# Expert layers: the hidden rows of two steps transposed together, the down products one step later

## The reference, cut to what matters

```python
def swiglu(h, w_gu, w_down):
    g, u = jnp.split(h @ w_gu, 2, axis=-1)
    return (jax.nn.silu(g) * u) @ w_down
...
# D_MODEL = 1024, SEQ = 256, N_EXPERTS = 8, TOP_K = 2, FFN_EXPERT = 3584
```

## Time and profile before

| | |
|---|---|
| median of 3 executions | 3080.19 us (3072.54, 3080.19, 3086.84) |
| the profiled execution | 3076.05 us, of it 3074.0 us span |
| TensorE busy | 2939.0 us, 96% of the span |
| VectorE busy, ScalarE busy | 1206.1 us (39%), 715.0 us (23%) |
| data read from HBM | 682.52 MB, 222 GB/s over the span |
| the expert stage | about 769 to 1740 us |
| mean granted clock of TensorE | 0.97 of full speed |

### The profile page before, as it was taken

How to read it: one execution, slowest core, us unless ns; L and a number is a source line. 1 busy time by engine, 2 the same in 40 slices (tenths; PEclk the granted TensorE clock), 3 DMA queues, 4 the chain that set the end, 5 groups by cost and what they waited for, 6 DMA issues and landing times.

```text
span 3074.0 us, 52144 instructions
## 1 busy us (share of the span) xinstructions
PE 2939.0 (96%) x23648; PEld 2023.6 (66%) x23648; DVE 1206.1 (39%) x2121; ACT 715.0 (23%) x1145; POOL 48.3 (2%) x39
## 2 busy tenths in 40 slices
PE   8888999998999999999999899899999999988898
PEld 6778988877233333333333466699999985687898
DVE  4767853242001111101101267455454543454454
ACT  2224432141000000000000111434334422311443
POOL 0000000000000000000000000000000000032000
PEclk9899999999999999999999999899999998998999
DMA  8756754537898999999999312046665331010452
GB/s 343 272 219 248 277 217 178 215 114 281 339 374 355 369 372 352 366 365 371 360 358 369 135 69 96 1 176 236 246 245 194 140 135 41 1 72 1 165 191 83
DMA packets 95204, 687.01 MB, mean 223 GB/s; under 512 B 10624, under 2 KB 11776, under 8 KB 11904
## 3 DMA queue, kind: packets, MB, share of 16 engines
q1 hardware_dynamic: 94400, 681.36, 57.6%
q10 hardware_dynamic: 576, 2.25, 0.2%
HBM read 682.52 MB, written 1.05 MB: 222 GB/s over the span
## 4 chain that ended last, share of the span: by engine, by line
PE 90%; DVE 5%; ACT 2%; DMA 1%; issue 1%; POOL 0%; SPq 0%; DVEq 0%; ACTq 0%
PE ps L493 40%; PE ps L1976 19%; PE ps L853 11%; PE ps L1999 7%; PE ps L764 5%; PE ps L2002 3%; PE ps L506 2%; PE ps L1984 1%; PE ps L739 1%; DMA ring<-W 1%; DVE FR L835 0%; DVE macc L609 0%; DMA XT<-XIN 0%; DVE AR L2472 0%; DMA sml<-SM 0%
## 5 line engine op out<-in xcount | busy, mean ns | idle before, releaser
L1976 PE MATMUL ps<-AR 128*32 128x512 f32 x4080 | 533.5, 592 | 0.0
L493 PE MATMUL ps<-HT,ring 128*128 128x256 f32 (+1 forms) x1696 | 443.4, 422 | 3.8 <-ACT HT L700 3.8
L493 PEld LDWEIGHTS ps<-HT,ring 128*128 128x128 f32 x1696 | 325.1, 193 | 115.4 <-issue 73.6
L493 PE MATMUL ps<-FR,FR 128*128 128x256 f32 x3120 | 390.1, 285 | 2.1 <-DVE M_moe_mod L617 1.7
L493 PEld LDWEIGHTS ps<-FR,FR 128*128 128x128 f32 x3120 | 379.8, 192 | 11.1 <-issue 8.6
L2087 DVE TENSOR_TENSOR AR<-AR,ps 128x256 f32<-128x256 f32 x84 | 35.5, 423 | 800.8 <-ACT AR L2051 800.8
L853 PE MATMUL ps<-FR,FR 128*128 128x256 f32 x2832 | 349.3, 283 | 0.0
L1976 PEld LDWEIGHTS ps<-AR 128*32 128x32 f32 x4080 | 150.7, 110 | 296.9 <-issue 294.5
L835 DVE TENSOR_TENSOR FR<-ring,FR 128x2048 fp32r<-128x2048 f32 x129 | 294.2, 2290 | 131.1 <-ACT FR L819 131.1
L853 PEld LDWEIGHTS ps<-FR,FR 128*128 128x128 f32 x2832 | 343.9, 192 | 0.8 <-issue 0.8
L819 ACT ACTIVATE FR<-ring 128x2048 fp32r<-128x2048 f32 x129 | 244.4, 1905 | 114.1 <-PE ps L853 86.7
(11 more groups left out here) (418 smaller groups left out, 2613.1 us busy)
## 6 DMA issues: line engine op xcount, KB each, us to landing
ring<-W SPq DMA_DIRECT2D x441, 1024.0 KB, 6.2
AR<-W SPq DMA_DIRECT2D x205, 1024.0 KB, 8.3
XT<-XIN ACTq DMA_DIRECT2D x2, 1024.0 KB, 8.6
cst<-CS SPq DMA_DIRECT2D x1, 1851.0 KB, 14.1
out<-XT SPq DMA_DIRECT2D x4, 256.0 KB, 2.2
sml<-SM SPq DMA_DIRECT2D x1, 970.5 KB, 10.2
cst<-CS ACTq DMA_DIRECT2D x1, 129.5 KB, 7.7
sml<-SM ACTq DMA_DIRECT2D x1, 16.0 KB, 5.2
```

The source lines that it names most:

```text
L493: ins = g.matmul(out, l, r, **kw)
L1976: ins = g.matmul(bank.ap[group(i), :], mo.hg[e % 2][:, 4 * h + k, group(t)], w[n][:, k, :], start=j == 0 and k == 0, stop=j == 1 and k == ...
```

## The change

Two consecutive steps' hidden rows are transposed together. The two `hu` buffers, 256 columns each, are read by one `turn` of four transposes at every second step (steps 2, 4, ..., 84), in place of two transposes at every step. They go to one PSUM bank, and one VectorE copy of 128x512 moves them into one half of a doubled buffer `hid2`, where the four `hid` buffers now are views. The down products of a round come three steps after its last piece and not two, so the loop has one step more, `scatter` comes one step later, and the `moe_d` loads move back by a step in SyncE's order. VectorE's `up` waits for the turn of the pair.

```diff
 def down_rounds(step):
-    return [n for n in range(ROUNDS) if last_up(n) == step - 2]
+    return [n for n in range(ROUNDS) if last_up(n) == step - 3]
...
     # expert_slots(), and the loops of TensorE, ScalarE and VectorE
-    for step in range(UPS + 2):
+    for step in range(UPS + 3):
...
-        mo.hid = [m_.get(256, "p (k j) -> p k j", k=2) for _ in range(4)]
+        mo.hid2 = [m_.get(512) for _ in range(2)]
+        mo.hid = [mo.hid2[i // 2][:, i % 2 * 256:i % 2 * 256 + 256].rearrange("p (k j) -> p k j", k=2) for i in range(4)]
...
         def scattered_at(e):
-            return last_up(14 * e + 13) + 4
+            return last_up(14 * e + 13) + 5
...
             # TensorE
             def turn(b):
                 bank = counts.take(p + ".turn", b)
-                s.wait_emptied(bank).wait_ge(p + ".hu", b)
-                for k in range(2):
-                    ins = g.transpose(bank.ap[:, k * 128:k * 128 + 128], mo.hu[b % 2][:, k * 128:k * 128 + 128], ident)
+                s.wait_emptied(bank).wait_ge(p + ".hu", b + 1)
+                for k in range(4):
+                    ins = g.transpose(bank.ap[:, k * 128:k * 128 + 128], mo.hu[k // 2][:, k % 2 * 128:k % 2 * 128 + 128], ident)
                 ins.then_inc(*s.done(p + ".turn", b))
             def down(n):
...
-                s.wait_ge(p + ".hd", last_up(n))
+                s.wait_ge(p + ".hd", last_up(n) // 2 * 2)
...
                 if step < UPS:
                     up(step)
-                if 1 <= step <= UPS:
-                    turn(step - 1)
+                if 2 <= step <= UPS and step % 2 == 0:
+                    turn(step - 2)
...
             # VectorE (its loop changes as TensorE's)
             def up(b):
                 s.wait_ge(p + ".sg", b)
                 if b >= 2:
-                    s.wait_ge(p + ".turn", b - 2)
+                    s.wait_ge(p + ".turn", (b - 2) // 2 * 2)
...
             def turn(b):
                 s.wait_ge(p + ".turn", b)
                 if b >= 4:
-                    s.wait_ge(p + ".down", (4 * (b - 4) + 3) // 3)
-                g.tensor_copy(mo.hid[b % 4], counts.bank(p + ".turn", b)[:, 0:256].rearrange("p (k j) -> p k j", k=2)).then_inc(
-                    *s.done(p + ".hd", b, empties=(p + ".turn", b)))
+                    s.wait_ge(p + ".down", (4 * (b - 3) + 3) // 3)
+                g.tensor_copy(mo.hid2[b % 4 // 2], counts.bank(p + ".turn", b)[:, :]).then_inc(*s.done(p + ".hd", b, empties=(p + ".turn", b)))
```

## The result

The changed kernel takes 3067.21 us (median of 11 executions, 3063.32 to 3071.11), the kernel before 3077.14 us (11 executions, 3070.36 to 3086.84). The ratio is 0.9966, with a 95% interval from 0.9954 to 0.9977: 0.34% faster, 10 us, with 7 to 14 us in the interval. I had forecast 7.7 us, and 3070.5 us. The profiled execution of the changed kernel has a span of 3065.7 us against 3074.0, 8.3 us less.

What follows compares the result with a forecast made beforehand. TensorE's instruction stream was taken to bound the expert stage; -12.2 + 2.8 + 1.7 = -7.7 us. This gave 3068.4 or 3072.5 us depending on the base, so 3070.5 us was forecast, range 3060 to 3081.

Steps and rivals of the forecast that it cites:

- a turn of two: TensorE's expert stage before the change: two transposes at a step, with the gap ahead of them, cost 0.51 us.
- a turn of four: TensorE's even steps after the change: four transposes cost 0.73 us, 0.22 more than two.
- gain in TensorE's stream: Expert stage: 84 turns of 0.51 us go and 42 of 0.73 come, -12.2 us.
- the delay and the moved loads: Down products and 112 `moe_d` loads one step later in SyncE's order: nothing moves, 0 us.
- the preparations behind that copy: VectorE's `prep` queued behind the larger copy, tightest at step 18: taken as nothing, bounds 0 and 1.4 us.
- wait for the accumulator bank: End of expert 0: `up(14)` takes the bank of `acc[0]` while ScalarE copies it out, +2.8 us once.
- half clock behind it: After expert 0's pause TensorE runs 3.3 to 3.4 us at 1.2 in place of 2.4 GHz, +1.7 us.
- the gap goes away with the transposes: Steps without a turn: down products follow up products at ordinary pace; otherwise 0.29 us stays in 42 steps.
- no stall: Rival, end of expert 0: the stall is hidden or absent, full -12.2 us, 3066 us; chance 0.12.
- It doesn't do what it says: Rival: the up-to-down gap stays in 42 steps without a turn, 0.29 us each, about 3082 us; chance 0.07.
- The stall at every end: Rival: every expert end but the last stalls with a clock fall, +19.3 us, about 3097 us; chance 0.04.
- The clock in the turns: Rival: each of 42 turns of four lets the clock fall, 71 us, about 3142 us; chance 0.01.

Runs made afterwards that it cites:

- the run with seven stalls: Changed kernel with the bank counter set, after experts 0 to 6, to that expert's first accumulator bank; 3087.50 us against 3078.17 for the kernel before, ratio 1.0030.
- the first experiment: Changed kernel with the bank counter moved on by two ahead of step 14, avoiding expert 0's accumulator banks; 3066.59 us against 3078.54 for the kernel before.
- eight in a row: Rows of four steps turned together, eight transposes every fourth step, one weight place less, no accumulator collision; 3055.31 us against 3078.17 for the kernel before.
- two turns in a row: Kernel before with the delay and two separate turns in even steps, bank counter moved on ahead of steps 24 and 66; 3066.11 us against 3078.54.

## Why the prediction was right, point by point

| step of the prediction | predicted | measured |
|---|---|---|
| a turn of two | 0.51 us | before: 9.95 - 9.44 |
| a turn of four | 0.73 us | 10.17 - 9.44 = 0.73 |
| a step without a turn | 9.44 us | 9.44 |
| gain in TensorE's stream | 12.2 us | 12.10 (stage without the stall) |
| the delay and the moved loads | 0 | 0.01 (stage) |
| VectorE's copy | 0.70 us, hidden | 0.68, hidden |
| the preparations behind that copy | 0 (at most 1.4 us) | 0: 5.9 us of idle weight loader ahead of their transposes in both kernels |
| wait for the accumulator bank | 2.8 us, once | 2.69, once |
| half clock behind it | 1.7 us | 1.73, the rest of 4.42; 1.70 from two up parts |
| sum | -7.7 us | -7.68 (stage) |

What carried it was the pace. An up part of 16 groups gave the price of a group, and two kinds of steps gave the turn's price with it. The row of waits would have misled: 70.4 us stand there for 84 gaps, and only 84 x 0.29 = 24 us of that could ever be had.

The step with the least ground was that the gap goes away with the transposes. No step of the kernel before showed up products followed by down products directly. The rows of down to up decided it, and the odd steps of the changed kernel show it.

The second was the bank. It is in no view of the profile of before, since there the wait doesn't exist. It came out of a walk through the allocation, and the price from the copies' rows. The place, the length and the one occurrence were right. Its clock term was right in this kernel but held for too sure: the run with seven stalls has the fall at three of seven. Had it not fallen, the sum would have been 9.4 us. That it fell at this pause, in the profiled execution, and the sum came out to 0.02 us, is in part luck.

The measured total moved by 10 us, not by 7.7. The forecast lies in the interval, 7 to 14 us. In the profiled executions the stage starts between 769.25 and 773.81 us, in nine kernels in which TensorE has the same work up to there. That is a scatter of 4.6 us ahead of TensorE's first changed step, more than the 2.3 us that differ. It goes with the clock outside the stage: of the changed kernel's eleven executions the three fastest (3063.3 to 3063.8 us) had a mean granted clock of 0.975, the two slowest (3071.0 and 3071.1 us) 0.970 and 0.971. That the 2.3 us are this scatter is likely and not shown. My 3070.5 us was 3.3 too high partly for its base, 3078.2, where eleven runs give 3077.1.

The rivals: *no stall* is the case of the first experiment, 4.4 us below what happened. *It doesn't do what it says* fell by the odd steps. *The stall at every end* needed the bank counter set by hand, and then cost 11.8 us over the kernel before in the stage (974.63 - 962.88), 9 us in the median. I had priced it at 19.3, with a clock fall each time. *The clock in the turns* fell with eight in a row.

## What to carry to other kernels

Where a stream of narrow-tile products is broken by wide-tile ones, count the places where the tile changes, and gather the wide work in few places; how many turns, banks or copies it makes doesn't matter as long as they are hidden. When a change alters how many banks are taken in turn, walk the allocation: a stall may be born where the next product lands on a bank that is just being copied out, and one line that moves the counter on takes it away. For an effect of a few tenths of a per cent, read the time of the stage in the trace; here two pairs of kernels with the same work for TensorE agree in it to 0.01 us, where the whole program scatters by 15 to 17.

## What the runs showed that I had not expected

At seven pauses of TensorE of the same 2.5 us the granted clock fell to 0.50 three times and stayed at 1.00 four times. The sharpest pair is the end of expert 0 and that of expert 4: the chain has the same pieces ahead of both pauses and behind both, and the clock fell after the first and not after the second. Nor is the moment fixed. At expert 0 the clock was still 1.00 in the first products behind the pause (914.1 to 914.8 us); at experts 1 and 5 it was below 1.00 before the products began again (0.87 in 1034.3 to 1034.7, 0.69 in 1526.0 to 1526.3). A pause of that length is therefore a risk of 1.7 us and not a price. What decides it isn't settled; no run here varied it.

The second is how exact the rest is. The kernel with two turns in a row and the one with joined turns have the same stage time, 950.78 us, though VectorE's work differs by 42 copies.
